# Hybrid attention / Mamba-2 layer: gate loads on ScalarE's queue, the residual in eight pieces, and a paired start of the attention output

## The chip, the cores and the metric

The kernel runs on one core of one Trainium2 chip. The metric is device microseconds (us) of one execution. TensorE (PE) multiplies, ScalarE (ACT) evaluates functions and copies, VectorE (DVE) and GpSimd (POOL) do elementwise work, and SyncE (SP) issues most of the transfers; ACT issues a few. A semaphore wait stops the whole in-order stream of the engine that waits.

## The reference

One layer (width 1024, float32) for a prompt of 1040 tokens and 8 single-token samples, which are computed together as 1048 columns. Everything ahead of `mixed` and behind it is the same before and after:

```python
x = x + 0.5 * swiglu(x, g_ffn1, w_ffn1_gate, w_ffn1_up, w_ffn1_down)
h = rmsnorm(x, g_mix)
q, k, v, qi, ki, wi, z, xbc, dt_raw, ga, gs = split(h @ w_in)
attn = attend(q, k, v, qi, ki, wi)              # sparse attention
ssd, ssm_state = ssd_mixer(xbc, dt_raw, z, h0)  # Mamba-2 scan, 2048 wide
mixed = sigmoid(ga) * (attn @ w_attn_out) + sigmoid(gs) * (ssd @ w_ssd_out)
x = x + mixed @ w_o
x = x + 0.5 * swiglu(x, g_ffn2, w_ffn2_gate, w_ffn2_up, w_ffn2_down)
```

## The kernel before

Activations lie transposed: 128 partitions x 8 blocks of width x 1048 columns, cut in three chunks of columns (352, 352, 344). A weight tile is 1024 x 128. SP loads it to `wraw` (`load_tile`), POOL splits it into a high and a low part (`split_tile`, lines 332 and 335, buffers `whi` and `wlo`, two slots each), and PE makes for each chunk 8 x 3 matmuls (high x high, low x high, high x low, lines 340 to 342) into PSUM set A or B, by the parity of the tile. The activation is split as well: ACT writes `hhi` (line 2199), DVE writes `hlo` (line 2204), a chunk at a time.

- `gemm_tile` does one tile, chunk by chunk. `gemm_pair` waits until both tiles of a pair are split (`w_split` at n + 2) and then does chunk 0 of both, chunk 1 of both, chunk 2 of both.
- A tile's split waits until the last chunk of the tile that used its slot (two tiles ago) is done.

The tail, behind the scan, has these stages, each of 8 tiles: **attention output** (AO), the two halves of the **SSD output** (SO1, SO2), **w_o** (WO). Then comes the norm and the second feed-forward.

The attention output runs beside the step of the samples' SSD state, one sample per tile. Per tile i and sample b = i the engines' orders, written out by hand, are:

- SP (`sp_tail`): load weight tile i + 2, wait for the new state `hn`, store it, wait for `ys` of sample b, load the old state `h0` and the rows `bcb` of sample b + 2.
- POOL (`pool_tail`): split tile i, then `bx` = outer product for sample b (line 2155; it waits for `bcb`).
- ACT (`act_tail`): 16 activations for the decay of sample b (`hn`, line 2219), then the three chunks of tile i from PSUM to `mixed` (line 2223), each behind its `gemm_done`.
- DVE (`dve_tail`): `hn` += `bx` (line 2261, needs the decay and `bx`), product with C (line 2264, written to h0's buffer), reduction to `ys` (line 2269).

When the eighth sample is through, `ys` is normalized and stored, and SO1's input `sraw` is loaded. In SO2 DVE mixes per tile and chunk (lines 2294 to 2299): mixed x gate, acc + PSUM, acc x gate, mixed + acc. The gates of tile m + 1 come into the same buffers (one per chunk) when chunk c of tile m has been mixed (`mix_ready`). All these loads are on SP's queue, in order with the weight tiles of SO2 and of WO; the residual `xre` (4192 KB, line 2122) is loaded in one transfer once `hlo` of SO2 has been written, between weight tiles 1 and 2. After the mixing, DVE writes `hlo` of WO, for which PE waits, and then adds the residual to each tile of WO.

Of the kernel before, what the change touches and what calls it, by code (L numbers as in the profile page):

```python
# [22 lines left out]
P = 128  # L23
D = 1024
KD = D // P
# [5 lines left out]
CH = [(0, 352), (352, 352), (704, T - 704)]  # L31
# [19 lines left out]
TILE_AO = TILE_IN + N_IN  # L51
# [5 lines left out]
ORD_AO = ORD_IN + N_IN // 2  # L57
# [25 lines left out]
def build(nc, A, O):  # L83
    ctx = ExitStack()
    with ctx:
# [169 lines left out]
        xD = nc.dram_tensor("xD", (D, T), F32).ap()  # L255
        zD = nc.dram_tensor("zD", (DI, T), F32).ap()
        gaD = nc.dram_tensor("gaD", (D, T), F32).ap()
        gsD = nc.dram_tensor("gsD", (D, T), F32).ap()
# [79 lines left out]
        def products(pe, out, w1, w2, r1, r2, start, stop):  # L338

            pe.matmul(out, w1, r1, start=start, stop=False)  # L340
            pe.matmul(out, w1, r2, start=False, stop=False)  # L341
            return pe.matmul(out, w2, r1, start=False, stop=stop)  # L342

        def gemm_tile(pe, n, q, slot, ready=None, free=True, between=None):

            pe.wait_ge(w_split, n + 1)
            for c, (o, w) in enumerate(CH):
                if ready is not None:
                    pe.wait_ge(ready[0], ready[1] + c + 1)
                if free:  # L350
                    pe.wait_ge(gemm_evac[slot], 3 * (q - 1) + c + 1)
                for k in range(KD):
                    mm = products(pe, SETS[slot][:, c, 0:w], whi[:, slot, bass.ts(k, P)],
                                  wlo[:, slot, bass.ts(k, P)], hhi[:, k, o:o + w], hlo[:, k, o:o + w],
                                  k == 0, k == KD - 1)
                mm.then_inc(gemm_done[slot], 1)
                if between is not None:
                    between(c)


        def gemm_pair(pe, n, q, ready, between=None):

            pe.wait_ge(w_split, n + 2)
            for c, (o, w) in enumerate(CH):
                if ready is not None:
                    pe.wait_ge(ready[0], ready[1] + c + 1)
                for j in range(2):
                    if q:
                        pe.wait_ge(gemm_evac[j], 3 * (q - 1) + c + 1)
                    for k in range(KD):  # L370
                        mm = products(pe, SETS[j][:, c, 0:w], whi[:, j, bass.ts(k, P)], wlo[:, j, bass.ts(k, P)],
                                      hhi[:, k, o:o + w], hlo[:, k, o:o + w], k == 0, k == KD - 1)
                    mm.then_inc(gemm_done[j], 1)
                if between is not None:
                    between(c)
# [1641 lines left out]
        gates = a.take("gates", [P, 3, 2, 352])  # L2017
# [12 lines left out]
        xre = at("xre", [P, KD, T], F32, AR)  # L2030
# [12 lines left out]
        part_ready = sem("part_ready")  # L2043
        sraw_loaded = sem("sraw_loaded")
        gates_loaded = [sem(f"gates_loaded{c}") for c in range(3)]
        mix_ready = sem("mix_ready")
        y_T, y_evac = sem("y_T"), [sem("y_evac_dve"), sem("y_evac_act")]
        PART_ORD = [ORD_AO, ORD_SO, ORD_SO + 4, ORD_WO]

        def sp_tail(sp):  # L2050
            ao = A["w_attn_out"][0].rearrange("(c h g p) n -> c h p g n", c=2, h=2, g=4)

# [55 lines left out]
            sp.wait_ge(part_ready, 6)  # L2108
            sp.dma_start(sraw[:, :, :], sD[D:2 * D, :].rearrange("(k p) t -> p k t", p=P)).then_inc(sraw_loaded, 16)

            def load_gates(m):
                for c, (o, w) in enumerate(CH):
                    if m:
                        sp.wait_ge(mix_ready, 3 * (m - 1) + c + 1)
                    for k, g_ in enumerate((gaD, gsD)):
                        sp.dma_start(gates[:, c, k, 0:w], g_[m * P:(m + 1) * P, o:o + w]).then_inc(gates_loaded[c], 16)
            load_gates(0)
            for m in range(KD):
                load_tile(sp, TILE_SO + KD + m, 0, m % 2, col_tile(so[D:2 * D, :], m * P))
                if m == 1:  # L2120
                    sp.wait_ge(part_ready, 9)
                    sp.dma_start(xre[:, :, :], xD.rearrange("(k p) t -> p k t", p=P)).then_inc(sraw_loaded, 16)
                if m >= 2:
                    load_gates(m - 1)
            load_gates(KD - 1)
            with sp.Fori(0, 4) as i:
                for j in range(2):
                    load_tile(sp, i * 2 + (TILE_WO + j), 0, j, col_tile(A["w_o"][0], i * 256 + j * P))
# [34 lines left out]
        def pe_tail(pe):  # L2163
            pe.wait_ge(smp_loaded, 96)
            for half in range(2):
                for k in range(4):
                    mm = pe.transpose(CD[half][0:NS, k * P:(k + 1) * P], xss[:, NXB + 4 * half + k, :], ident[:, :])
                mm.then_inc(bct_done, 1)
            for m in range(KD):
                gemm_tile(pe, TILE_AO + m, ORD_AO + m // 2, m % 2, ready=(part_ready, 0) if m == 0 else None)  # L2170
            pe.wait_ge(smp_dve, 2)
            pe.matmul(bankC[:, 0:NXB * NS], ones[:, :], ysr[:, :, :].rearrange("p k b -> p (k b)"),
                      start=True, stop=True).then_inc(ys_ss, 1)
            for s in (1, 2, 3):
                n, q = (TILE_AO + 8 * s, PART_ORD[s])
                for m in range(2):
                    gemm_tile(pe, n + m, q, m, ready=(part_ready, 3 * s) if m == 0 else None)
                with pe.Fori(0, 3 if s < 3 else 2) as i:
                    for j in range(2):
                        gemm_tile(pe, i * 2 + (n + 2 + j), i + (q + 1), j)  # L2180
            gemm_pair(pe, TILE_FFN2 - 2, ORD_FFN2 - 1, None, (lambda c: pe_sumsq(pe, 2, c - 1) if c else None))
            pe_ffn(pe, 1)
            pe.wait_ge(down_evac, 48 * NI)
            for t in range(NT):
                o, _, w = trow(t)
                if t >= 2:
                    pe.wait_ge(y_evac[0], t - 1)
                    pe.wait_ge(y_evac[1], t - 1)
                for k in range(KD):
                    mm = pe.transpose(SETS[t % 2][0:w, k // 4, k % 4 * P:(k % 4 + 1) * P], X[:, k, o:o + w], ident[:, :])  # L2190
                mm.then_inc(y_T, 1)

        def act_part(act, s, src, ready):

            for c, (o, w) in enumerate(CH):
                act.wait_ge(ready[0], ready[1] + ready[2] * c)
                if s:
                    act.wait_ge(gemm_done[1], 3 * (PART_ORD[s] - 1) + c + 1)
                act.activation(hhi[:, :, o:o + w], src[:, :, o:o + w], ACT.Identity).then_inc(part_hi, 1)
# [5 lines left out]
                                ALU.subtract).then_inc(part_ready, 1)  # L2205

        def act_tail(act):
            act_part(act, 0, qT, (over, 15, 0))
            act.wait_ge(smp_loaded, 96)
            act.activation(smb[:, 1, :, :], smb[:, 1, :, :], ACT.Exp).then_inc(smp_act, 1)  # L2210
            act.wait_ge(smp_act, 1)
            for i in range(KD):
                b, s = i, i % 2

                act.wait_ge(h0_loaded[s], 16 * (b // 2) + 16)
                if b >= 2:
                    act.wait_ge(slot_out[s], 16 * (b // 2) + HN_OUT0[s])
                for k in range(NXB):
                    ins = act.activation(hn[:, s, k, :], h0[:, s, k, :], ACT.Identity, scale=smb[:, 1, k, b:b + 1])
                ins.then_inc(h0_decayed, 1)  # L2220
                for c, (o, w) in enumerate(CH):
                    act.wait_ge(gemm_done[s], 3 * (ORD_AO + i // 2) + c + 1)
                    act.activation(mixed[:, i, o:o + w], SETS[s][:, c, 0:w], ACT.Identity).then_inc(gemm_evac[s], 1)
            act.wait_ge(ys_ss, 2)
            act.activation(rss[:, :, :], rss[:, :, :], ACT.Sqrt, bias=eps[:, 0:1], scale=1.0 / GW).then_inc(smp_act, 1)
            act_part(act, 1, sraw, (sraw_loaded, 16, 0))
            for i in range(KD):
                for c, (o, w) in enumerate(CH):
                    act.wait_ge(gemm_done[i % 2], 3 * (ORD_SO + i // 2) + c + 1)
                    act.activation(acc[:, i, o:o + w], SETS[i % 2][:, c, 0:w], ACT.Identity)\  # L2230
                        .then_inc(gemm_evac[i % 2], 1)
            act_part(act, 2, sraw, (sraw_loaded, 32, 0))
            act_part(act, 3, mixed, (mix_ready, 3 * (KD - 1) + 1, 1))
            act_norm(act, 2)
            act_ffn(act, 1)
            y_copy(act, 1)
# [12 lines left out]
        def dve_tail(v, ch):  # L2249
# [48 lines left out]
                    ch.run(v.tensor_tensor(acc[:, m, cs], acc[:, m, cs], gates[:, c, 1, 0:w], ALU.mult))  # L2298
                    v.tensor_tensor(mixed[:, m, cs], mixed[:, m, cs], acc[:, m, cs], ALU.add).then_inc(mix_ready, 1)
            dve_part(v, 3, mixed)  # L2300
            v.wait_ge(sraw_loaded, 48)
            def residual(m, c):
                o, w = CH[c]
                v.wait_ge(gemm_done[m % 2], 3 * (ORD_WO + m // 2) + c + 1)
# [130 lines left out]
```

## Time and profile before

| what | value |
|---|---|
| median of 3 runs (lowest to highest) | 4030.69 us (4028.98 to 4035.45) |
| profiled execution: its own time | 4030.77 us |
| profiled execution: span | 4029.2 us |
| mean granted clock of TensorE | 0.926 |
| PE busy | 3610.1 us, 90% of the span |
| DVE / POOL / ACT busy | 2223.3 / 1454.2 / 792.5 us |
| chain that ended last | PE 73%, DVE 11%, issue 4%, POOL 3%, ACT 3%, DMA 2% |

Windows and starts are in us from the start of the span. In a row of the timeline the first number is the start, the second the time from start to end of the merged instructions, then engine, line, operation, output<-input, shape and count; in brackets stands how long the engine was idle before it and what released it. "issue" names no releaser. A line of the windows gives busy time and count of each engine, then the granted clock, the DMA share and GB/s.

### The profile page before, as it was taken

How to read it: one execution, taken by the hardware profiler on the slowest of the kernel's cores; microseconds unless marked ns; L12 is line 12 of the kernel's file. 1: busy time of each engine (PE TensorE's matmuls, PEld its weight loads, DVE VectorE, ACT ScalarE, POOL GpSimd, SP SyncE). 2: the span in 40 equal slices, each digit the busy share in tenths (PEclk: the TensorE clock that was granted, in tenths of full speed). 3: DMA queues.
4: the chain of work that ended last, by engine and by line, in shares of the span. 5: the costliest groups of instructions: out<-in, count | busy, mean ns of one | idle time of the engine just before them, and what ended most of it. 6: DMA issues, size and time to landing. Idle time of an engine off the chain costs nothing.

```text
span 4029.2 us, 59114 instructions
## 1 busy us (share of the span) xinstructions
PE 3610.1 (90%) x22349; PEld 3413.2 (85%) x22349; DVE 2223.3 (55%) x3820; ACT 792.5 (20%) x1644; POOL 1454.2 (36%) x641
## 2 busy tenths in 40 slices
PE   4999999989999999883799869885798989999998
PEld 3999999988869999883689657664798989999998
DVE  4333333455758899998556535896618143343434
ACT  2000000022321111112565204663310010000000
POOL 1453535323324444340110005774633343435341
PEclk7999999999989999996799866996899999999999
DMA  3111111122112222211100104655725111111111
GB/s 65 48 57 32 57 36 52 41 74 50 43 37 89 95 92 82 79 63 57 46 1 1 38 10 126 182 138 139 211 94 161 32 51 33 57 36 52 42 47 58
DMA packets 419888, 272.47 MB, mean 68 GB/s; under 512 B 82071, under 2 KB 395599, under 8 KB 419735
## 3 DMA queue, kind: packets, MB, share of 16 engines
q1 hardware_dynamic: 380900, 234.43, 20.6%
q10 hardware_dynamic: 38870, 36.47, 2.7%
q8 instruction: 74, 1.21, 0.1%
q14 instruction: 44, 0.36, 0.0%
HBM read 211.14 MB, written 59.91 MB: 67 GB/s over the span
## 4 chain that ended last, share of the span: by engine, by line
PE 73%; DVE 11%; issue 4%; POOL 3%; ACT 3%; DMA 2%; SPq 2%; ACTq 1%; DVEq 0%; POOLq 0%
PE setA L340 8%; PE setA L341 8%; PE setA L342 8%; PE setB L340 7%; PE setB L341 7%; PE setB L342 7%; PE bankC L340 2%; PE bankC L342 2%; PE bankC L341 2%; PE bankD L342 2%; PE bankD L340 2%; PE bankD L341 2%; DVE sc L1045 2%; DVE top L1042 2%; PE bankC L1261 2%
## 5 line engine op out<-in xcount | busy, mean ns | idle before, releaser
L332 POOL TENSOR_TENSOR whi<-wraw,ones 128x1024 fp32r<-128x1024 f32 x192 | 465.4, 2424 | 1753.3 <-PE setA L342 1111.7
L340 PE MATMUL setA<-hhi,whi 128*128 128x352 f32 (+1 forms) x2304 | 763.0, 331 | 99.7 <-issue 49.2
L341 PE MATMUL setA<-hlo,whi 128*128 128x352 f32 (+1 forms) x2304 | 754.4, 327 | 0.0
L340 PE MATMUL setB<-hhi,whi 128*128 128x352 f32 (+1 forms) x2304 | 747.7, 325 | 5.8 <-POOL wlo L335 5.8
L342 PE MATMUL setA<-hhi,wlo 128*128 128x352 f32 (+1 forms) x2304 | 752.7, 327 | 0.0
L341 PE MATMUL setB<-hlo,whi 128*128 128x352 f32 (+1 forms) x2304 | 743.4, 323 | 0.0
L342 PE MATMUL setB<-hhi,wlo 128*128 128x352 f32 (+1 forms) x2304 | 742.2, 322 | 0.0
L340 PEld LDWEIGHTS setA<-hhi,whi 128*128 128x128 f32 x2304 | 443.9, 193 | 110.0 <-issue 56.4
L335 POOL TENSOR_TENSOR wlo<-wraw,whi 128x1024 fp32r<-128x1024 f32 x192 | 488.9, 2546 | 15.0
L341 PEld LDWEIGHTS setA<-hlo,whi 128*128 128x128 f32 x2304 | 443.8, 193 | 2.0
L342 PEld LDWEIGHTS setA<-hhi,wlo 128*128 128x128 f32 x2304 | 443.3, 192 | 0.0
L340 PEld LDWEIGHTS setB<-hhi,whi 128*128 128x128 f32 x2304 | 434.4, 189 | 10.2 <-POOL wlo L335 6.7
L341 PEld LDWEIGHTS setB<-hlo,whi 128*128 128x128 f32 x2304 | 434.1, 188 | 1.6
L342 PEld LDWEIGHTS setB<-hhi,wlo 128*128 128x128 f32 x2304 | 434.0, 188 | 0.0
L634 DVE SCALAR_TENSOR_TENSOR X<-bankC,X 128x352 f32<-128x352 f32 (+1 forms) x240 | 125.3, 522 | 466.8 <-PE bankC L342 466.8
L605 ACT ACTIVATE sg<-setA 128x352 f32<-128x352 f32 x132 | 60.9, 463 | 1364.0 <-PE setA L342 1364.0
L620 DVE TENSOR_TENSOR hidf<-sg,setB 128x352 f32<-128x352 f32 x132 | 67.9, 515 | 344.0 <-PE setB L342 343.4
L1042 DVE MAX8 top<-sc 128x8 f32<-128x384 f32 (+6 forms) x224 | 210.5, 940 | 32.3 <-issue 31.7
L1045 DVE MATCH_REPLACE8 sc<-top,sc 128x384 f32<-128x384 f32 (+6 forms) x224 | 207.1, 924 | 0.0
L634 DVE SCALAR_TENSOR_TENSOR X<-bankD,X 128x352 f32<-128x352 f32 (+1 forms) x240 | 125.3, 522 | 104.4 <-PE bankD L342 104.4
L340 PE MATMUL bankC<-hidhi,whid 128*128 128x352 f32 (+1 forms) x528 | 171.1, 324 | 9.9 <-DVE hidlo L625 7.0
L342 PE MATMUL bankC<-hidhi,wlod 128*128 128x352 f32 (+1 forms) x528 | 171.0, 324 | 0.0
(413 smaller groups left out, 5938.7 us busy)
## 6 DMA issues: line engine op xcount, KB each, us to landing
wraw<-in_w_in SPq DMA_DIRECT2D x64, 512.0 KB, 3.7
wraw<-in_w_ffn_gate SPq DMA_DIRECT2D x44, 512.0 KB, 3.8
wraw<-in_w_ffn_up SPq DMA_DIRECT2D x44, 512.0 KB, 3.8
wraw<-in_w_ffn_down SPq DMA_DIRECT2D x44, 512.0 KB, 3.5
abc<-acsD SPq DMA_DIRECT2D x8, 2048.0 KB, 9.9
xcD<-cv ACTq DMA_DIRECT2D x24, 520.0 KB, 2.7
xc<-xcD SPq DMA_DIRECT2D x8, 1536.0 KB, 14.6
zD<-spill ACTq DMA_DIRECT2D x16, 524.0 KB, 2.7
```

What stands on the lines that cost most here:

```text
L332: pool.tensor_tensor(dst_cols(slot, hi), dst_cols(slot), ones[:, :].unsqueeze(1).to_broadcast([P, KD, P]), ALU.mult).then_inc(w_hi, 1)
L335: pool.tensor_tensor(lo[:, slot, :], wraw[:, slot, :], hi[:, slot, :].bitcast(F32), ALU.subtract).then_inc(w_split, 1)
L340: pe.matmul(out, w1, r1, start=start, stop=False)
L341: pe.matmul(out, w1, r2, start=False, stop=False)
L342: return pe.matmul(out, w2, r1, start=False, stop=stop)
L605: act.activation(sg[:, o:o + w], setA[:, c, 0:w], ACT.Silu).then_inc(gemm_evac[0], 1)
L620: v.tensor_tensor(hidf[:, o:o + w], sg[:, o:o + w], setB[:, c, 0:w], ALU.mult)\
L634: v.scalar_tensor_tensor(X[:, m, o:o + w], CD[u % 2][:, 0:w], 0.5, X[:, m, o:o + w], ALU.mult, ALU.add).then_inc(down_evac, 1)
L1042: v.max(t8, s_).then_inc(topk_step, 1)
L1045: v.match_replace(s_, t8, s_, TAKEN).then_inc(topk_step, 1)
L1261: mm = pe.transpose(CD[bank][0:kn, b * P:(b + 1) * P], pr[:, u % 2, (b0 + b) * P:(b0 + b) * P + kn], ident[:, :])
```

## The change

The gates are issued by ACT: those of tile 0 behind ACT's last copy of SO1 and ahead of its part of SO2's input, those of tiles 1 to 7 behind that part, each still behind its `mix_ready`. The residual is issued in eight pieces of 524 KB on SP's queue, the first seven behind weight tiles 1 to 7 of SO2 and the last behind those; DVE waits for all eight. Tiles 0 and 1 of the attention output go through `gemm_pair` rather than `gemm_tile`. The orders of POOL, of ACT in the attention output and of DVE are not edited.

```diff
+        def load_residual(sp, k):
+            sp.dma_start(xre[:, k, :], xD[k * P:(k + 1) * P, :]).then_inc(sraw_loaded, 16)
...
-            def load_gates(m):
-                for c, (o, w) in enumerate(CH):
-                    if m:
-                        sp.wait_ge(mix_ready, 3 * (m - 1) + c + 1)
-                    for k, g_ in enumerate((gaD, gsD)):
-                        sp.dma_start(gates[:, c, k, 0:w], g_[m * P:(m + 1) * P, o:o + w]).then_inc(gates_loaded[c], 16)
-            load_gates(0)
             for m in range(KD):
                 load_tile(sp, TILE_SO + KD + m, 0, m % 2, col_tile(so[D:2 * D, :], m * P))
                 if m == 1:
                     sp.wait_ge(part_ready, 9)
-                    sp.dma_start(xre[:, :, :], xD.rearrange("(k p) t -> p k t", p=P)).then_inc(sraw_loaded, 16)
-                if m >= 2:
-                    load_gates(m - 1)
-            load_gates(KD - 1)
+                if m >= 1:
+                    load_residual(sp, m - 1)
+            load_residual(sp, KD - 1)
...
-            for m in range(KD):
-                gemm_tile(pe, TILE_AO + m, ORD_AO + m // 2, m % 2, ready=(part_ready, 0) if m == 0 else None)
+            gemm_pair(pe, TILE_AO, ORD_AO, (part_ready, 0))
+            for m in range(2, KD):
+                gemm_tile(pe, TILE_AO + m, ORD_AO + m // 2, m % 2)
...
         def act_tail(act):
+            def load_gates(m):
+                for c, (o, w) in enumerate(CH):
+                    if m:
+                        act.wait_ge(mix_ready, 3 * (m - 1) + c + 1)
+                    for k, g_ in enumerate((gaD, gsD)):
+                        act.dma_start(gates[:, c, k, 0:w], g_[m * P:(m + 1) * P, o:o + w]).then_inc(gates_loaded[c], 16)
...
+            load_gates(0)
             act_part(act, 2, sraw, (sraw_loaded, 32, 0))
+            for m in range(1, KD):
+                load_gates(m)
             act_part(act, 3, mixed, (mix_ready, 3 * (KD - 1) + 1, 1))
...
-            v.wait_ge(sraw_loaded, 48)
+            v.wait_ge(sraw_loaded, 32 + 16 * KD)
```

## Rows read from the trace of the kernel before

**Rows 1.** Windows: the attention output from its third tile on, and all of SO2

```profile
2811.00:2884.00 73.00, 69.92 (x432) 68.47 (x430) 62.76 (x21) 36.67 (x116) 62.75 (x16) 1.00 0.84 234
...
3012.00:3107.00 95.00, 94.62 (x576) 94.23 (x576) 74.92 (x95) 2.56 (x1) 33.75 (x14) 0.97 0.53 169
```

**Rows 2.** Timeline of PE: starts of AO tiles 0 and 1, of SO2, of WO

```profile
2779.11 0.64 PE L340 MATMUL setA<-hhi,whi 128*128 128x352 f32 x1
...
2796.56 0.66 PE L340 MATMUL setB<-hhi,whi 128*128 128x352 f32 x1 [4.52 <-POOL wlo L335]
...
3012.15 0.63 PE L340 MATMUL setA<-hhi,whi 128*128 128x352 f32 x1 [8.01 <-issue]
...
3117.27 0.63 PE L340 MATMUL setA<-hhi,whi 128*128 128x352 f32 x1 [10.12 <-issue]
```

**Rows 3.** Timeline of POOL: bx of sample 0 to the split of tile 2

```profile
2786.16 3.65 POOL L2155 TENSOR_TENSOR bx<-bcb,smb 128x2048 f32<-128x2048 f32 x1 [20.36 <-DMA bcb<-bcD]
...
2792.24 4.27 POOL L335 TENSOR_TENSOR wlo<-wraw,whi 128x1024 fp32r<-128x1024 f32 x1
2796.47 5.69 POOL L2155 TENSOR_TENSOR bx<-bcb,smb 128x2048 f32<-128x2048 f32 x1
2802.12 2.39 POOL L332 TENSOR_TENSOR whi<-wraw,ones 128x1024 fp32r<-128x1024 f32 x1
```

**Rows 4.** Timeline of ACT: decay of sample 1, then tile 1's three chunks

```profile
2792.43 4.77 ACT L2219 ACTIVATE hn<-h,smb 128x128 f32<-128x128 f32 x16
2803.28 0.47 ACT L2223 ACTIVATE mixed<-setB 128x352 f32<-128x352 f32 x1 [6.08 <-PE setB L342]
...
2810.94 0.46 ACT L2223 ACTIVATE mixed<-setB 128x344 f32<-128x344 f32 x1 [3.33 <-PE setB L342]
```

**Rows 5.** Groups by line, 2779 to 2884: the two-input operations of DVE and POOL

```profile
L2155 POOL TENSOR_TENSOR bx<-bcb,smb 128x2048 f32<-128x2048 f32 x8 | 38.8, 4844 | 25.1 <-DMA bcb<-bcD 25.0
...
L2264 DVE TENSOR_TENSOR h<-hn,bcb 128x2048 f32<-128x2048 f32 x8 | 32.8, 4095 | 0.3
...
L2261 DVE TENSOR_TENSOR hn<-hn,bx 128x2048 f32<-128x2048 f32 x8 | 31.2, 3904 | 20.6 <-POOL bx L2155 16.2 <-ACT hn L2219 4.5
...
L335 POOL TENSOR_TENSOR wlo<-wraw,whi 128x1024 fp32r<-128x1024 f32 x7 | 30.1, 4306 | 0.6
...
L332 POOL TENSOR_TENSOR whi<-wraw,ones 128x1024 fp32r<-128x1024 f32 x7 | 16.8, 2397 | 0.0
```

**Rows 6.** Timeline of DVE: ys of sample 1, and sample 7 with POOL idle

```profile
2811.10 2.29 DVE L2269 TENSOR_REDUCE ys<-h 128x16 f32<-128x2048 f32 x1
...
2876.92 2.29 DVE L2261 TENSOR_TENSOR hn<-hn,bx 128x2048 f32<-128x2048 f32 x1 [1.32 <-POOL bx L2155]
```

**Rows 7.** The chain that ended last: loads of bcb, first pair and sample 3

```profile
2782.00 4.02 DMA bcb<-bcD
...
2814.24 8.01 DMA bcb<-bcD
```

**Rows 8.** Start of SO2: ACT's issue cost, POOL's split and DVE's low parts

```profile
L963 ACTq DMA_DIRECT2D xcD<-cv x24: 338/339/348, 1560.1 to 1873.4; - x24
...
3006.74 2.37 POOL L335 TENSOR_TENSOR wlo<-wraw,whi 128x1024 fp32r<-128x1024 f32 x1
...
3007.11 10.88 DVE L2204 TENSOR_TENSOR hlo<-sraw,hhi 128x2816 fp32r<-128x2816 f32 x3 [91.75 <-ACT hhi L2199]
```

**Rows 9.** Timeline of DVE: mixing beside a split, tiles 5 and 7, then hlo

```profile
3084.20 0.51 DVE L2296 TENSOR_TENSOR acc<-acc,setB 128x344 f32<-128x344 f32 x1 [1.57 <-PE setB L342]
3084.75 2.34 DVE L2298 TENSOR_TENSOR acc<-acc,gates 128x344 f32<-128x344 f32 x1
3087.12 2.60 DVE L2299 TENSOR_TENSOR mixed<-mixed,acc 128x344 f32<-128x344 f32 x1
...
3114.09 9.02 DVE L2204 TENSOR_TENSOR hlo<-mixed,hhi 128x2816 fp32r<-128x2816 f32 x3
```

**Rows 10.** The tile gates: from issue to landing, min/median/max

```profile
DMA to landing us min/median/max: 2.1/2.6/13.8
```

## Prediction

> **What bounds the kernel now.** I read the windows first, then PE's gaps, then in each gap the engines that PE waits for. TensorE is busy 90% of the span, so an edit can only pay, or cost, where PE stands still. The change touches three stages. In SO2 PE is busy 94.62 of 95 us [rows 1], so nothing that speeds its weights, gates or mixing shortens it; what counts is its start and the start of WO. PE stands still 8.01 us ahead of SO2 and 10.12 us ahead of WO [rows 2]. In the attention output PE is busy 69.92 of 73 us too [rows 1], yet it isn't what sets that stage's end: there POOL is busy 62.75 and DVE 62.76 us of the same 73.
>
> What sets it is seen by putting the durations of one form side by side. DVE's `hn` takes 2.29 us while POOL is idle [rows 6], but 3.90 on average, and 4.10 for the other two-input product [rows 5]; POOL's low part takes 2.37 us alone [rows 8] and 4.31 here; `bx` takes 3.65 alone and 5.69 when it starts inside a DVE product [rows 3]. So a two-input operation of one engine waits for that of the other. At their durations alone, the stage holds 8 x 3.65 (bx) + 16 x 2.29 (DVE's two products) + 7 x 2.39 + 7 x 2.37 (splits) = 99 us of such work, and it lies between the first bx at 2786.2 and the last product at 2876.92 + 2 x 2.29 = 2881.5 [rows 3, 5, 6], 95 us. The turn-taking between DVE and POOL is full from the first sample to the last. **Time in which neither works is not got back.** A second limit runs beside it: from the end of `ys` of sample 1 (2811.10 + 2.29) to the arrival of `bcb` for sample 3 (2814.24 + 8.01) pass 8.86 us [rows 6, 7], and bx of sample 3 needs it.
>
> The Trainium skill (SBUF — State Buffer, the section on why SBUF has two sides) says that the port pair shared by VectorE and GpSimd is an exclusive lock held for the whole instruction. The trace agrees (2.29 against 4.1). By the lock the stage has no slack, as in my sum; by mere mutual slowing, which could ease when the engines meet less, the third rival below would be the forecast.
>
> **The change part by part.**
>
> 1. **Pair at AO's start, on PE.** Before, tile 0 starts at 2779.11 with only its own split done, and tile 1 at 2796.56, 4.52 us after tile 0's end, since POOL does bx of sample 0 first and only then the split of tile 1, whose low part ends at 2796.5 [rows 2, 3]. A pair waits for both splits, and POOL's order is unchanged: the pair starts at 2796.56. PE's 13 us of tile 0 ahead of that are given up. One start at the lower clock instead of two gives back little: tile 1's first chunk took 2803.28 - 2796.56 = 6.7 us, where a chunk later takes (2810.94 - 2803.28) / 2 = 3.83 [rows 4], so 2.9 us of PE; it isn't PE that sets the end.
>
> 2. **What waits for tile 0's last chunk.** In a pair the chunks alternate: A0, B0, A1, B1, A2, B2. A0 is done at 2803.28, A2 four chunks later, at 2803.28 + 4 x 3.83 = 2818.6 (before: a little under 2792.43, where ACT went on). Two engines stand behind A2. POOL's split of tile 2 needs set A's slot; before, it ran at 2802.12, straight behind bx of sample 1 [rows 3]. ACT has three copies of tile 0 ahead of the decay of sample 1, which before ran at 2792.43 and takes 4.77 us [rows 4], so it now ends at 2819 + 4.8 = 2823.8, and `hn` of sample 1 on DVE waits for it. Hence from 2802.1 to 2818.6 neither DVE nor POOL has a two-input operation: **+16.5 us**.
>
> 3. **The load loop behind it.** From 2818.6 the order is whi and wlo of tile 2, bx of sample 2, hn 1, whi of tile 3, product 1, then `ys` 1: 3 x 2.4 + 3.65 + 3 x 2.3 = 17.8, so `ys` 1 ends at 2836.4. SP's next loads, h0 and bcb of sample 3, stand behind that: bcb lands at 2836.4 + 8.86 = 2845.3. Meanwhile the shared work runs dry at 2836.4 - 2.3 + wlo 3, hn 2, product 2 (7.0) = 2841.1. **+4.2 us** until bx of sample 3. From there both limits run as before: carried on in the same way, the sum has bx of sample 5 find its bcb in time, by some 2 us. Sum for the stage: **+20.7**. Bounds: bcb in 4.02 us from its issue, as the first pair did [rows 7], leaves 0.2 of the 4.2, so +16.7; 13.8 us, the longest landing of a gate load [rows 10], gives +26.4. I take 8.01, the same transfer in the same stage. PE follows: from tile 2 on it needs 3 x 3.83 = 11.5 us a tile, and the shared work 99 / 8 = 12.4 a sample. What comes behind `ys` 7, the store and the load of `sraw`, moves by the same amount.
>
> 4. **Gates of tile 0 on ACT ahead of SO2's high part.** Six issues stand between ACT's last copy and the conversion for which DVE and then PE wait. ACT issues a transfer in 0.338 us [rows 8], with what lies between them about 0.4: 2.4 us later. But DVE's three low parts took 10.88 us here against 9.02 undisturbed [rows 8, 9]; the 1.9 more came from POOL's split, which ended at 3006.74 + 2.37 = 3009.1 [rows 8]. Started 2.4 us later, the first low part misses it. **+0.5**; from 0 (hidden whole) to +2.4 (nothing given back). Gates 0 land some 2.6 us after issue [rows 10], long before DVE mixes.
>    Gates 1 to 7 stand on ACT behind waits for `mix_ready`; behind them is only the conversion for WO, which needs later mixing anyway: nothing.
>    The Trainium skill (DMA: Bandwidth & Descriptors, Issuing engines are not separate DMA queues) holds that another issuing engine saves only the time of issuing. No run here shows it yet; by it the gates' landing gains nothing from ACT's queue.
>
> 5. **Residual in eight pieces.** SO2's weight tile 2 no longer stands behind 4192 KB, so its split comes earlier. PE had no gap there [rows 1]: 0 on PE. The cover is tiles 0 and 1, 23 us of PE; without it the late split would have cost.
>
> 6. **w_o's weights earlier.** SP no longer waits for mixing before the loads of w_o. The first split then falls behind the second last tile's end, where DVE catches up in time, and the second starts when SO2's last chunk is done (3117.27 - 10.12 = 3107.15) and still meets the last mixing. The nearest picture is tile 5: from PE's end to the last mixing result 3087.12 + 2.60 - 3084.20 = 5.5 us beside a split [rows 9]. So 3107.15 + 5.5, plus one low part (9.02 / 3 = 3.0) and 0.1 is 3115.75, against 3117.27: **-1.5**. If no split met it, three operations of 0.53 and a low part would give 3111.9, -5.4; if the meeting is as bad as now, 0.
>
> Sum: 20.7 + 0.5 - 1.5 = **+19.7 us**. The profiled execution took 4030.77 us (span 4029.2), 0.08 above the median of the runs, so 4050.5. Bounds together: 16.7 + 0 - 5.4 = +11.3 (4042) and 26.4 + 2.4 + 0 = +28.8 (4060). A measurement of this kernel can tell about 0.2%, 8 us, from no change.
>
> **Rivals.**
>
> - **The samples stay bunched** (0.08). After the late start samples 2 and 3 come in step, and the 4.2 us of waiting for `bcb` return for samples 5 and 7: 16.5 + 3 x 4.2 - 1.0 = +28.1, 4058.9. For it: my margin of 2 us there is small, and the DMA share is already 0.84 [rows 1]. Against: the shared work refills between them.
> - **Not slower** (0.05). If tile 1's split were done by about 2780, tile 0's last chunk in a pair would be done by 2802.1, when POOL first wants it, and the stage would end as now; left are +0.5 - 1.5 = -1.0, 4029.8. Point of decision: whether bx of sample 0 really stands ahead of that split. POOL's rows show it starting first, at 2786.16 [rows 3], so I see little for it.
> - **The stage catches up to PE** (0.08). If DVE and POOL only hinder each other by chance, the stage could run at PE's pace from tile 2: split at 2818.6 + 4.8 = 2823.4, six tiles of 11.5, end 2892.4 against `ys` 7's 2881.5 + 2.3 = 2883.8 before: +8.6 - 1.0 = +7.6, 4038.4. Against: 99 us of work in 95 [rows 3, 5, 6].
>
> **How the numbers follow.** The forecast case, with its bounds 4042 to 4060, has 0.79, and the bunched case lies in the same range. I leave out the other two, 0.13 with some room for what I missed: range 4042 to 4060. Faster by over 0.2%: 0.02. Within 0.2%: the not-slower case and part of catching up, 0.07. Slower: 0.91.
>
> **What would show it.** Right: in the changed profile, PE's first matmul of AO at 2796 to 2797 with both sets alternating; an empty stretch of 16 us on POOL and DVE up to 2818.6; the decay of sample 1 at 2819; a wait of bx of sample 3 for bcb; `ys` of sample 7 near 2904.5 instead of 2883.8; the gaps ahead of SO2 near 8.5 and ahead of WO near 8.6; no gap in SO2. Wrong: the pair starting at 2779, a POOL split of tile 2 before 2815, or the end of `ys` 7 before 2895.

## The result and the profile after

Over five runs the changed kernel takes a median of 4052.36 us (4048.99 to 4053.92), the kernel before 4030.80 (4028.98 to 4035.45). The ratio is 1.0048 with a 95% interval of 1.0036 to 1.0060: slower by half a per cent. 4050.5 was predicted. The profiled execution took 4049.14 us with a span of 4047.3, 18.1 above that of before.

The timeline of POOL in the attention output, which answers to [rows 3]; the first number is the start, the second the duration:

```profile
2783.96 3.64 POOL L2151 TENSOR_TENSOR bx<-bcb,smb 128x2048 f32<-128x2048 f32 x1 [20.33 <-DMA bcb<-bcD]
...
2794.20 5.69 POOL L2151 TENSOR_TENSOR bx<-bcb,smb 128x2048 f32<-128x2048 f32 x1
2816.68 2.40 POOL L332 TENSOR_TENSOR whi<-wraw,ones 128x1024 fp32r<-128x1024 f32 x1 [16.79 <-PE setA L342]
...
2844.17 3.64 POOL L2151 TENSOR_TENSOR bx<-bcb,smb 128x2048 f32<-128x2048 f32 x1 [10.22 <-DMA bcb<-bcD]
```

ACT's timeline in the same stretch, which answers to [rows 4]:

```profile
2801.23 0.47 ACT L2227 ACTIVATE mixed<-setA 128x352 f32<-128x352 f32 x1 [20.98 <-PE setA L342]
2808.93 0.47 ACT L2227 ACTIVATE mixed<-setA 128x352 f32<-128x352 f32 x1 [7.23 <-PE setA L342]
2816.57 0.46 ACT L2227 ACTIVATE mixed<-setA 128x344 f32<-128x344 f32 x1 [7.18 <-PE setA L342]
2816.93 4.78 ACT L2223 ACTIVATE hn<-h,smb 128x128 f32<-128x128 f32 x16
```

And DVE's:

```profile
2821.80 5.50 DVE L2268 TENSOR_TENSOR hn<-hn,bx 128x2048 f32<-128x2048 f32 x1 [23.09 <-ACT hn L2223]
...
2831.74 2.29 DVE L2276 TENSOR_REDUCE ys<-h 128x16 f32<-128x2048 f32 x1
...
2836.26 2.29 DVE L2271 TENSOR_TENSOR h<-hn,bcb 128x2048 f32<-128x2048 f32 x1
...
2902.15 2.29 DVE L2276 TENSOR_REDUCE ys<-h 128x16 f32<-128x2048 f32 x1
```

POOL stands still 16.79 us for tile 0's last chunk, DVE 23.09 us for the decay of sample 1, which ACT makes only behind its third copy of tile 0, and later POOL stands still 10.22 us for `bcb`. The **stage**, from the start of `bx` 0 to the end of `ys` 7, takes 2904.4 - 2784.0 = 120.5 us, against 2883.8 - 2786.2 = 97.7 before: +22.8.

PE's timeline at the starts of the pair, SO2 and WO, which answers to [rows 2]:

```profile
2794.29 0.66 PE L340 MATMUL setA<-hhi,whi 128*128 128x352 f32 x1 [17.19 <-POOL wlo L335]
...
3032.72 0.63 PE L340 MATMUL setA<-hhi,whi 128*128 128x352 f32 x1 [8.72 <-issue]
...
3134.97 0.63 PE L340 MATMUL setA<-hhi,whi 128*128 128x352 f32 x1 [8.54 <-issue]
```

The gap ahead of SO2 grows from 8.01 to 8.72 us (+0.7), that ahead of WO shrinks from 10.12 to 8.54 (-1.6). SO2 has no gap in the changed kernel; before there was one of 0.23 us, ahead of its third tile.

### The profile page after: what moved, and what is told of

The parts are those of the page before. It is cut to its first block, busy times and chain, and to the rows that moved or that the text cites. A ratio compares the mean times of both kernels' runs of the same rounds, so it can differ in the third digit from the quotient of the medians.

```text
span 4047.3 us, 59120 instructions
## 1 busy us (share of the span) xinstructions
PE 3604.0 (89%) x22349; PEld 3408.6 (84%) x22349; DVE 2219.5 (55%) x3820; ACT 791.8 (20%) x1644; POOL 1450.9 (36%) x641
## 4 chain that ended last, share of the span: by engine, by line
PE 74%; DVE 12%; issue 5%; ACT 4%; POOL 3%; DMA 1%; ACTq 1%; SPq 1%; DVEq 0%; POOLq 0%
PE setA L340 8%; PE setA L341 8%; PE setA L342 8%; PE setB L340 8%; PE setB L341 8%; PE setB L342 8%; PE bankC L340 2%; PE bankC L342 2%; PE bankC L341 2%; PE bankD L342 2%; PE bankD L340 2%; PE bankD L341 2%; DVE sc L1045 2%; DVE top L1042 2%; DVE cv L1086 2%
```

## Experiments

Twelve kernels ran. e1 to e4 shared their runs of the kernel before (median 4031.1 us), so did e5 to e7 (4030.6) and e8 to e11 (4031.1); e12 had its own (4031.4). The ratios are to these. "Stage" is the stretch from bx 0 to ys 7, read as above.

**e1, no pair.** The changed kernel with the old loop of `gemm_tile` in the attention output.

```diff
-            gemm_pair(pe, TILE_AO, ORD_AO, (part_ready, 0))
-            for m in range(2, KD):
+            for m in range(KD):
```

> The changed kernel with tiles 0 and 1 of the attention output taken one after the other again; gates on ACT and the residual in pieces stay. My theory (the pair alone costs; the other edits move only the starts of SO2 and WO): the samples' last ys ends 20 to 23 us earlier than with the pair, the gap ahead of SO2 is 8.7 us, that ahead of WO 8.6, no gap in SO2, and the time is that of before less 1, so 4029 to 4031 us. Rival (loads on ACT's queue or the residual in pieces carry a good part of the loss): 4036 us or more.

Measured: 4029.98 us, ratio 0.9996 (0.9987 to 1.0005). Stage 97.5 us; gaps 8.72 and 8.54.

**e2, the pair alone**, the opposite edit on the kernel before.

> The kernel before with nothing but the pair. My theory: the whole loss, 4052 to 4054 us, the samples' stage longer by 21 to 23 us, the gaps ahead of SO2 and WO as before, 8.0 and 10.1 us. Rival (parts of the change work together for the loss): clearly under 4048 us.

Measured: 4053.65 us, ratio 1.0056 (1.0042 to 1.0070). Stage 120.4 us; gaps 8.01 and 10.44. The two runs agree: the pair carries the loss; gates and residual together are worth at most 0.13%. e2 also shows the cover of the residual at its edge: with the pair but the old single transfer of 4192 KB, PE has a gap of 0.77 us in SO2 (0.23 in the kernel before, none in the changed one), whose third tile's weights POOL got only then. The row is the split of that tile:

```profile
3055.18 2.39 POOL L332 TENSOR_TENSOR whi<-wraw,ones 128x1024 fp32r<-128x1024 f32 x1 [23.74 <-DMA wraw<-in_w_ssd_out]
```

**e3, the pair with an early second split; e4, the same without the pair.** In both POOL splits tile 1 straight behind tile 0, in the 20 us in which it waits for the first `bcb`.

```diff
+            split_ao(0)
+            split_ao(1)
             for i in range(KD):
-                split_tile(pool, TILE_AO + i, ...)
+                if i >= 2:
+                    split_ao(i)
```

> The changed kernel, pair included, with POOL splitting tile 1 straight behind tile 0, ahead of bx of sample 0, where POOL idles 20 us. My theory (it is the lateness of tile 0's last chunk that costs, not the pair's order of chunks): PE starts near 2777 to 2779, tile 0's last chunk is done near 2801, the split of tile 2 follows at once, and the whole loss goes: 4026 to 4031 us. Rival (the alternation itself starves the samples, since ACT copies tile 0 over a longer time): 4038 us or more.

Measured: 4026.83 us, ratio 0.9988 (0.9979 to 0.9997). Stage 96.0 us. With the second split done in time the pair costs nothing: its order of chunks is harmless, its wait for both splits is not.

> As e1, with tile 1 split ahead of bx of sample 0. My theory (DVE's and POOL's two-input operations take turns and fill the stage, so 4.7 us of them moved out of it shorten it by that): 4.5 us under e1, about 4025 us, and ys of sample 7 ends 4 to 5 us earlier relative to bx of sample 0. Rival (the stage is paced by the load of bcb or by PE): no more than 1 us under e1.

Measured: 4029.36 us, ratio 0.9995 (0.9986 to 1.0004). Stage 97.3 us, against 97.5 in e1. **This expectation failed:** 4.7 us of the work in which DVE and POOL take turns left the stage, and it is 0.2 us shorter, within what its rival allowed (1 us). POOL's timeline of e4 shows what was there in its place:

```profile
2786.32 7.26 POOL L2156 TENSOR_TENSOR bx<-bcb,smb 128x2048 f32<-128x2048 f32 x2 [12.75 <-DMA bcb<-bcD]
...
2810.96 3.65 POOL L2156 TENSOR_TENSOR bx<-bcb,smb 128x2048 f32<-128x2048 f32 x1 [8.55 <-DMA bcb<-bcD]
```

bx of sample 2 starts at 2810.96, in the kernel before at 2811.09: the load of its `bcb` comes when it did, and POOL waits 8.55 us for it.

**e5, decay of sample 1 ahead of ACT's copies of tile 0; e6, also bx of sample 2 ahead of the split of tile 2; e8, also the decay of sample 2 between ACT's first and second copy.** All three keep the pair and its late start. e5's edit on ACT:

```diff
+            decay(0)
+            decay(1)
             for i in range(KD):
-                (decay of sample i)
+                if i >= 2:
+                    decay(i)
                 (three copies of tile i)
```

> The changed kernel, pair included, with ACT making the decay of sample 1 ahead of its copies of tile 0. My theory: hn and product of sample 1 (4.6 us of turn-taking work) go into the empty stretch, and ys of sample 1 is early enough for the load of bcb of sample 3, so that bx of sample 3 does not wait; what stays is 16.5 - 4.6 = 12 us of the loss: 4041 to 4043 us. Rival (only POOL's late split counts): no change, 4052 us. Rival (only ACT's late decay counts): back to 4030 us.

Measured: 4040.15 us, ratio 1.0026 (1.0016 to 1.0037). Stage 109.0 us: half the loss is gone, about what was expected (4041 to 4043).

> As e5, and POOL makes bx of sample 2 ahead of the split of tile 2. My theory: another 3.65 us of the work fills the empty stretch: 8 us of the loss stay, 4037 to 4039 us. Rival (the split of tile 2 is what counts, through PE): as e5.

Measured: 4039.76 us, ratio 1.0023 (1.0013 to 1.0033). Stage 109.1: nothing gained on e5, where 4037 to 4039 was expected; the rival "as e5" holds.

> As e6 (pair; decay of sample 1 and bx of sample 2 ahead), and ACT also makes the decay of sample 2 between its first and second copy of tile 0. In e6 hn of sample 2 waited 17.4 us for that decay, which stood behind the copies of both tiles of the pair. My theory (ACT's order hands the pair's lateness on): hn and product of sample 2 go into the empty stretch, and the stage, 109.1 us from bx 0 to ys 7 in e6, gets 4 to 9 us shorter; 4031 to 4036 us. Rival (POOL's splits of tiles 2 and 3 set it): as e6, 4040 us.

Measured: 4041.11 us, ratio 1.0025 (1.0015 to 1.0034). Stage 108.3, where 4 to 9 us less than in e6 were expected. Again nothing, though both moves did what they should: hn of sample 2 no longer waits 17.4 us as in e6, and then hn of sample 3 does, in e8's timeline of DVE:

```profile
2812.13 2.29 DVE L2278 TENSOR_TENSOR hn<-hn,bx 128x2048 f32<-128x2048 f32 x1 [4.64 <-POOL bx L2152]
...
2838.97 2.29 DVE L2278 TENSOR_TENSOR hn<-hn,bx 128x2048 f32<-128x2048 f32 x1 [19.91 <-ACT hn L2225]
```

What bounds it now is in the window of e8 from the pair's start to the end of tile 7 (busy time and count of PE, weight loads, DVE, ACT, POOL, then granted clock, DMA share, GB/s):

```profile
2794.80:2891.80 97.00, 95.28 (x576) 94.46 (x576) 63.23 (x23) 37.94 (x119) 66.14 (x19) 0.97 0.72 205
```

PE is busy 95.28 of 97 us; in the same stretch of e5 and e6 it is busy 94.4 of 97.5 and 94.2 of 97.2. Each tile's copies, and behind them the next decay, go at PE's pace, and PE started 17 us late. e5, e6 and e8 all end within 1 us of each other; that PE's pace is the floor under them is read from these windows, no run moved it. It is the rival "catches up to PE" as the price of the pair, +10.6 of stage (108.3 against 97.7); the other 12.2 us of the loss came through ACT's order and the load of `bcb`.

**e7, high parts on ACT.** As e4, and ACT converts the weights of tiles 2 to 7 (`whi`) behind its copies of the tile two before; POOL is left with `wlo`.

```diff
+                if i + 2 < KD:
...
+                    act.activation(whi[:, s, :], wraw[:, s, :], ACT.Identity).then_inc(w_hi, 1)
```

> As e4 (no pair, tile 1 split early), with the high parts of tiles 2 to 7 of the attention output made by ACT rather than POOL: the same values, 6 x 2.4 = 14 us less of the work in which POOL and DVE take turns. My theory: DVE's hn takes clearly under 3.9 us on average, and the stage is now paced by PE (11.5 us a tile) instead of 12.4: it ends 3 to 4 us earlier than in e4, about 4022 us. Rival (DMA or the load of bcb paces it): as e4 within 1 us, or slower through ACT's longer order.

Measured: 4027.64 us, ratio 0.9994 (0.9984 to 1.0004). Stage 93.7 us, 3.6 less than e4 as expected, but the time, expected at about 4022, is not. DVE's hn takes 2.73 us on average. From the groups by line of e7, to be held against [rows 5]:

```profile
L2286 DVE TENSOR_TENSOR hn<-hn,bx 128x2048 f32<-128x2048 f32 x8 | 21.9, 2734 | 38.6 <-ACT hn L2235 27.4 <-POOL bx L2164 11.2
L2289 DVE TENSOR_TENSOR h<-hn,bcb 128x2048 f32<-128x2048 f32 x8 | 20.4, 2554 | 0.3
```

The same instruction on DVE gets shorter by 1.2 to 1.5 us when POOL has less to do: what slows DVE is POOL's work. Of the 3.6 us the run times show little: the medians differ by 1.7 us, each against its own runs of before by 1.2, and the intervals of the ratios overlap. Behind the stage e4, e7, e9 and e11 all lose 2 us that the kernel before doesn't: POOL's first split of SO1's weights meets DVE's last product of `ys`, a 128x128 one, and makes it 2.3 to 2.4 us from 0.29. In e7:

```profile
L2309 DVE TENSOR_TENSOR ys<-ys,gssd 128x128 f32<-128x128 f32 x1 | 2.3, 2311 | 0.0
```

**e10, bcb first without the pair; e11, bcb first with it.** SP issues `bcb` of sample b + 2 as soon as the product of sample b is done, ahead of h0.

```diff
                 if b + 2 < NS:
+                    sp.wait_ge(ys_done, 2 * b + 1)
+                    load_bc(b + 2)
                     load_h0(b + 2)
-                    load_bc(b + 2)
```

> As e4 (no pair, tile 1 split early), and SP issues the load of bcb of sample b + 2 as soon as the product of sample b is done, ahead of the load of h0. e4 took 4.7 us of turn-taking work out of the stage without shortening it. Theory A (the loop through bcb held it there): bcb comes 3 to 5 us earlier, and the stage shortens by 3 to 5 us, to 93 to 94 us. Theory B (the steady turn-taking of 12.4 us a sample holds it, and the start does not matter): unchanged, 97 us, with bcb waiting ready.

Measured: 4026.09 us, ratio 0.9989 (0.9979 to 0.9998). Stage 94.8 us, 2.6 less than e4. That is theory A, a little smaller than expected. (The interval of the ratio overlaps that of e4, so the gain is read from the stage.) bx of sample 2, in POOL's timeline of e10:

```profile
2802.19 4.16 POOL L2157 TENSOR_TENSOR bx<-bcb,smb 128x2048 f32<-128x2048 f32 x1 [1.61 <-DMA bcb<-bcD]
```

It now waits 1.61 us instead of 8.55. What is late next is h0, and with it the decays (six waits of ACT for it, 21.6 us).

> The changed kernel, pair included, with bcb loaded first as in e10. It tests the term of 4.2 us by itself (bx of sample 3 waiting for bcb; 10.2 us of POOL's idle time ahead of it in the profile). Theory: bx of sample 3 starts 3 to 5 us earlier, as much comes off the stage of 120.5 us, about 4048 us; the 16.5 us stay. Rival (h0 behind it and its decay on ACT take over as the wait): under 1.5 us gained.

Measured: 4048.22 us, ratio 1.0043 (1.0028 to 1.0058). Stage 117.1 us, 3.4 less than in the changed kernel; POOL's wait for the `bcb` of sample 3 falls from 10.22 to 1.65 us. Counted from bx 0, bx of sample 3 starts 8.9 us earlier, where 3 to 5 were expected, yet only 3.4 come off the stage: the decay of sample 3 waits for h0 and begins 56.6 us behind bx 0 in both kernels, and hn of sample 3 now waits for it. The load order has a price in this kernel. How much of it belongs to the pair this run doesn't tell, since the same edit takes 2.6 us off without the pair (e4 to e10).

**e9, splits behind the first low part.** As e3; the gates of tile 0 behind ACT's conversion, and two of POOL's splits wait for the first low part.

```diff
-            pool_rest(pool, TILE_SO, ORD_SO, 12)
+            for t in range(24):
+                if t == 9:
+                    pool.wait_ge(part_ready, 7)
+                if t == 17:
+                    pool.wait_ge(part_ready, 10)
+                split_tile(pool, TILE_SO + t, ...)
```

> As e3 (pair, tile 1 split early), the gates of tile 0 issued behind ACT's conversion instead of ahead of it, and POOL's split of the second tile of SO2 and of w_o made to wait until the first low part of that stage is written, so that it meets neither the low part nor the last mixing. My theory: the gap ahead of SO2 goes from 8.7 to about 6.1 us and that ahead of WO from 8.5 to about 5; 6 us under e3, 4021 us. Rival (the later split makes PE wait for tile 1, or meets the other low parts at the same price): no gain.

Measured: 4020.61 us, ratio 0.9973 (0.9963 to 0.9984), **the lowest median of the study**: it beats both the kernel before and the changed one (1.0048). Gaps 6.16 and 4.76 us. Ahead of WO the 3.8 us come from the held split alone. Ahead of SO2 two edits meet: the kernel before, with no gates there and the split not held, has 8.01, so by that row 0.7 of the 2.56 us is the gates' and 1.85 the split's. The last mixing and the low parts of WO in its timeline of DVE, against [rows 9]:

```profile
3106.05 0.51 DVE L2312 TENSOR_TENSOR acc<-acc,setB 128x344 f32<-128x344 f32 x1 [0.82 <-PE setB L342]
3106.59 0.52 DVE L2314 TENSOR_TENSOR acc<-acc,gates 128x344 f32<-128x344 f32 x1
3107.14 0.52 DVE L2315 TENSOR_TENSOR mixed<-mixed,acc 128x344 f32<-128x344 f32 x1
3107.58 11.20 DVE L2211 TENSOR_TENSOR hlo<-mixed,hhi 128x2816 fp32r<-128x2816 f32 x3
```

The mixing takes 1.6 us instead of 5.5. The split now meets the second and third low part (11.20 us for the three instead of 9.02), for which PE isn't waiting.

**e12, all of it together**, without the pair.

> A version that takes what the runs so far showed to pay: no pair, tile 1 split ahead of bx of sample 0, the high parts of tiles 2 to 7 on ACT (e7), bcb loaded first (e10), the two splits held until the first low part is written and the gates of tile 0 behind the conversion (e9), and the first split of SO1's weights held until ys is normalized, since in e4, e7 and e9 it met DVE's last small product (2.3 to 2.4 us instead of 0.3). Theory: the stage comes to PE's own time, 8 tiles of 11.5 us and 2.9 us of one start at the lower clock from 7 us ahead of bx 0, so about 90 us from bx 0 to ys 7 against 96.1 in e9, 2 us less behind it, gaps of 6.2 and 4.8 us ahead of SO2 and WO: 4013 us. Rival (with PE the bound, the samples' work falls behind its last tile instead): stage above 93 us, 4016 us or more.

Measured: 4024.57 us, ratio 0.9983 (0.9974 to 0.9992). Stage 99.2 us: **the expectation failed and the rival's numbers hold**; its picture too, since PE's last tile is done 8.1 us ahead of the end of `ys` 7, in the kernel before 0.9. e9 keeps the lower median, but the two intervals overlap. Two of e12's waits in the stage (engine and line, what for, us in total, times, longest), and its hn among the groups by line:

```profile
ACT whi L2253 <- DMA wraw<-in_w_attn_out: 30.6, 5, 7.2
...
DVE hn L2293 <- ACT hn L2243: 16.9, 6, 4.4
...
L2293 DVE TENSOR_TENSOR hn<-hn,bx 128x2048 f32<-128x2048 f32 x8 | 29.3, 3663 | 26.7 <-ACT hn L2243 16.9 <-POOL bx L2165 9.8
```

ACT converts weights ahead of a decay and waits 5 to 7 us for them each time. That can't be the whole cause, for e7 has the same wait in a stage of 93.7 us:

```profile
ACT whi L2245 <- DMA wraw<-in_w_attn_out: 27.0, 5, 8.0
```

What differs is what DVE's products take beside POOL: hn takes 3.66 us on average (2.73 in e7), the other product 3.80 (2.55). Two edits that shortened the stage alone (e7, e10) cancel; by which of these ways is open, since e12 puts all these edits together and no run takes one out. The small product behind the stage is back at 0.29 us, and the two gaps are 6.16 and 4.75.

## Why the prediction was right

- **Step 1 (the pair starts when both splits are done)** holds: PE's first matmul at 2794.29 lies 10.3 us behind bx 0, where [rows 2, 3] have tile 1 at 10.4. e3, which has the pair without the wait, loses nothing.
- **Step 2 (+16.5)**: POOL stood still 16.79 us, and DVE had no two-input operation in it either. Right by 0.3.
- **Step 3 (+4.2)** was too small. The shared work ran dry at 2836.26 + 2.29 = 2838.6 and bx of sample 3 came at 2844.17: 5.6 us. The load took 2844.17 - (2831.74 + 2.29) = 10.1 us from the end of `ys` 1 instead of 8.86. With 16.8 that makes 22.4 of the 22.8 measured; 20.7 was said. The delay isn't kept whole, as the prediction has it: counted from bx 0 it is 24.1 us at bx of sample 3 and 22.6 at that of sample 7. e11 takes the wait away and gains 3.4 us, of which an unknown part would be gained without the pair too. The upper bound should have read +26.5 by its own terms, not +26.4.
- **Step 4 (+0.5)**: +0.7, and for the reason given: six issues took 2.45 us, POOL's split ended at 3028.9, the first low part began at 3029.5, and the three took 9.03 us instead of 10.88. The gates landed no sooner: the median is 4.0 us, 2.6 before, beside the pieces of the residual. **Step 5 (0)**: no gap in SO2; [rows 1] hid one of 0.23 us. **Step 6 (-1.5)**: -1.6, by the same meeting of split and mixing, 5.4 us from PE's end to the last result where 5.5 was said; e9 takes the meeting away and gets a gap of 4.76 us, which is the low end of that step (10.12 - 5.4 = 4.7).
- **Where the reasoning was wrong though the number held:** "The turn-taking between DVE and POOL is full from the first sample to the last. Time in which neither works is not got back." e4 took 4.7 us of it out for nothing. In the first samples the load of `bcb` sets the time, and e10, which loads it earlier, gains 2.6 us; from about sample 3 on the turn-taking counts too (e7). The sum of 99 us in 95 should have warned me: operations that take strict turns can't fill less than their sum. At a hand-over the two overlap a little. In the kernel before, the split of tile 2 ends at 2802.12 + 2.39 = 2804.51 [rows 3], and DVE's hn, which started beside it, ends 2.16 us later, less than its 2.29 alone:

```profile
2802.30 4.37 DVE L2261 TENSOR_TENSOR hn<-hn,bx 128x2048 f32<-128x2048 f32 x1 [1.31 <-POOL bx L2155]
```

  Limits of nearly the same length lay side by side, and I read them as one. The forecast depended little on it, since the pair's idle time stands ahead of both.
- **The third rival** was dismissed with too little: PE's pace isn't what the kernel settles to, but it is a floor, and with the pair's late start it lies 10.6 us up (e5, e6, e8). It was near before, too: the decay of sample 7, which ACT makes behind tile 6's copies, ended at 2875.7, and three operations of 2.3 us behind it give 2882.6 as an estimate, 1.3 us under the measured end of `ys` 7. My expectations for e6 and e8 left it out.

The sum was +19.7; the medians differ by 21.6, the profiled spans by 18.1. The stage gave +22.8, the two gaps -0.9. As far as is known, no part of the rest follows from the change: the profiled execution was 2.2 us ahead when bx 0 began (2783.96 against 2786.16), three of PE's starts were 3 us shorter, below, and 1.4 us the other way are not traced. That the profiled execution lies so near the forecast is luck; the median is 1.9 us above it, much as step 3 was too small. e2, with nothing but the pair, is 22.6 us above its own runs of before.

## What to carry to other kernels

Before pairing two tiles, look at when the second tile's input is ready and at who is waiting for the first tile's end: a pair moves that end from half to five sixths of the pair's time, and every in-order engine with other work behind it hands the delay on. Where a stage seems filled by one resource, take some of that work out and see whether it shortens: two loops of nearly the same length look like one. Order is cheap to change: delaying two splits until they could no longer meet an operation that PE waits for, and moving six issues behind a conversion, gained 6.2 us (e3 to e9), more than the new load order (e10) or the conversions on ACT (e7). Edits that gain alone may cancel when put together (e12).

## What was not expected of the hardware

- **PE's starts.** At SO1, SO2 and WO the same first 26 matmuls behind a gap took 6.5 to 6.9 us in the kernel before and 5.6 to 5.7 in the one after, with granted clocks of 0.58 to 0.60 and 0.70 to 0.71. At SO2 and WO, before and after:

```profile
3012.15:3018.61 6.46, 6.46 (x26) 6.46 (x27) 6.28 (x4) 0.00 (x0) 0.00 (x0) 0.60 0.01 3
3117.27:3124.12 6.85, 6.85 (x26) 6.85 (x27) 5.84 (x3) 0.00 (x0) 0.00 (x0) 0.58 0.00 0
```

```profile
3032.72:3038.40 5.68, 5.68 (x26) 5.68 (x27) 5.68 (x2) 1.61 (x1) 0.00 (x0) 0.71 0.01 3
3134.97:3140.65 5.68, 5.68 (x26) 5.68 (x27) 5.68 (x2) 0.00 (x0) 0.00 (x0) 0.70 0.00 0
```

  PE stays longer or shorter at its lower level (1.2 GHz), which makes 0.8 to 1.2 us a start and 3 us over these three, and no edit explains it. The changed kernel isn't always the quicker: at its pair the 26 matmuls took 6.9 us at a clock of 0.55. In the other kernels they took 5.6 to 6.9 us, and behind the same gap of 8.72 us 5.7 (e3) as well as 6.2 (e1). The Trainium skill (TensorE: Matmul & The Clock Gate, the section What's actually happening) says that the point of the change varies from run to run; the runs agree, and it bounds how finely two profiles can be compared.
- **A small product can be held for a large one.** 128x128 on DVE, 0.29 us, took 2.31 us beside a split on POOL in e7 and e4, and 0.29 in e12, which holds that split back. Eight times its length isn't a sharing of speed; it fits waiting for the end of the other engine's instruction, a split part of 2.4 us.
- **Six transfers on ACT's queue take 2.45 us of ACT** (0.39 to 0.45 each; step 4 had 2.4), as ACT's timeline of the changed kernel has it ahead of the conversion. In e9 they stand behind it in the order, and the issues (3006.47 to 3009.27) ran beside the first conversion, which began at 3006.57:

```profile
3026.39 0.45 ACTq L2211 DMA_DIRECT2D gates<-gsD  x1
3026.95 7.38 ACT L2196 ACTIVATE hhi<-sraw 128x2816 fp32r<-128x2816 f32 x3 [2.45 <-issue]
```
